# Gated DeltaNet stage: masks ahead of queries on GpSimd, identity and edge masks by bf16 products into PSUM, decay matrix by eight exponentials with a bias

## The reference

```
g = cumsum(log_alpha)
decay = masked_exp(tri_incl, g[:, None] - g[None, :])
L = where(tri_strict, (k * beta) @ k.T * decay, 0)
Tm = inverse of (I + L)
v_new = Tm @ (v * beta) - Tm @ (k * beta * exp(g)) @ S
o = (q * exp(g)) @ S + (q @ k.T * decay) @ v_new
S = S * exp(g_last) + (k * exp(g_last - g)).T @ v_new
```

## Time and profile before

| | before |
|---|---|
| median of 3 runs | 2450.79 us (2449.39 to 2457.24) |
| the profiled execution's own time | 2452.5 us |
| its span, first to last instruction | 2450.7 us |
| PE, PE weight loads, DVE, ACT, POOL busy | 87%, 54%, 60%, 52%, 31% of the span |
| mean granted clock of PE | 0.94 of 2.4 GHz |
| GDN stages | 372.5 to 512.5 us and 1443.5 to 1583.2 us |

### The profile page before, as it was taken

How to read it: one execution, slowest core, us unless ns; L and a number is a source line. 1 busy time by engine, 2 the same in 40 slices (tenths; PEclk the granted TensorE clock), 3 DMA queues, 4 the chain that set the end, 5 groups by cost and what they waited for, 6 DMA issues and landing times.

```text
span 2450.7 us, 54596 instructions
## 1 busy us (share of the span) xinstructions
PE 2143.4 (87%) x23078; PEld 1334.2 (54%) x23078; DVE 1462.0 (60%) x1822; ACT 1284.6 (52%) x1664; POOL 750.9 (31%) x557
## 2 busy tenths in 40 slices
PE   5998987878989999999898878888969999999990
PEld 3765656755565555555765557654644444444440
DVE  2256735559362121215567665386379999999976
ACT  3443753456534242423533654465268877887862
POOL 0422115332314242423232234333122333333321
PEclk8999987998999999999999888898979999999995
DMA  9222990020212222316220000020276677990023
GB/s 276 98 88 73 309 293 11 3 56 4 72 52 86 69 88 66 103 51 176 81 93 24 1 10 3 3 57 22 92 255 212 224 269 277 329 317 35 27 104 137
DMA packets 215385, 278.46 MB, mean 114 GB/s; under 512 B 28177, under 2 KB 188797, under 8 KB 215039
## 3 DMA queue, kind: packets, MB, share of 16 engines
q1 hardware_dynamic: 203776, 243.60, 30.9%
q0 software_dynamic: 8432, 29.89, 3.3%
q10 hardware_dynamic: 2959, 1.83, 0.3%
HBM read 368.35 MB, written 29.11 MB: 162 GB/s over the span
## 4 chain that ended last, share of the span: by engine, by line
PE 52%; issue 16%; DVE 14%; POOL 8%; ACT 7%; DMA 3%; SPq 1%; POOLq 0%; DVEq 0%; ACTq 0%
PE ps L2268 49%; POOL mix L968 5%; DVE arena L1662 2%; DMA wbuf<-in_w_mod 1%; DVE mix L1670 1%; DVE mix L1662 1%; PE ps L2475 1%; ACT arena L1142 1%; DVE mix L1666 1%; DVE const L1662 1%; DVE yg L1662 1%; DVE hT L1662 1%; DVE xT L1662 1%; POOL mix L971 1%; DVE arena L1666 1%
## 5 line engine op out<-in xcount | busy, mean ns | idle before, releaser
L2268 PE MATMUL ps<-hT,mix 128*128 128x512 f16 (+2 forms) x3024 | 380.0, 288 | 25.1 <-DVE hT L1662 15.2
L2268 PE MATMUL ps<-w,xgT 128*128 128x512 f16 x1632 | 365.4, 381 | 7.3 <-DVE w L2163 7.3
L2268 PEld LDWEIGHTS ps<-hT,mix 128*128 128x128 f16 x3024 | 230.0, 99 | 172.8 <-issue 19.5
L2163 DVE SCALAR_TENSOR_TENSOR w<-wst,w 128x2048 f16<-128x2048 f32 x136 | 310.0, 2320 | 22.7 <-ACT w L1523 22.7
L1000 POOL TENSOR_TENSOR a<-aval,a 128x256 f16<-128x256 f32 x68 | 159.0, 2338 | 371.1 <-ACT a L1571 371.1
L2268 PEld LDWEIGHTS ps<-w,xgT 128*128 128x128 f16 x1632 | 157.4, 98 | 186.0 <-issue 10.5
L1523 ACT ACTIVATE w<-wst 128x2048 f16<-128x2048 f32 x136 | 251.5, 1899 | 6.4 <-DMA xs_rows<-htok,slot_i 6.4
L2268 PE MATMUL ps<-mix 128*128 128x512 f16 (+5 forms) x1856 | 203.5, 286 | 14.5 <-POOL mix L971 8.8
L2268 PE MATMUL ps<-hT,arena 128*128 128x128 f16 (+1 forms) x1440 | 201.2, 301 | 1.1 <-DVE const L1662 1.1
L2268 PE MATMUL ps<-w2m,aT 128*128 128x512 f16 x816 | 188.7, 381 | 5.5 <-DVE aT L2201 5.5
L2268 PEld LDWEIGHTS ps<-mix 128*128 128x128 f16 (+3 forms) x1856 | 120.3, 122 | 88.4 <-POOL mix L971 12.4
(11 more groups left out here) (360 smaller groups left out, 3604.5 us busy)
## 6 DMA issues: line engine op xcount, KB each, us to landing
wst<-in_moe_w SPq DMA_DIRECT2D x204, 1024.0 KB
wbuf<-in_w_mod SPq DMA_DIRECT2D x40, 1024.0 KB
wbuf<-in_ffn_w SPq DMA_DIRECT2D x33, 1024.0 KB
wbuf<-in_w_in SPq DMA_DIRECT2D x20, 1024.0 KB
xs_rows<-in_table SPq DMA_DIRECT2D x17, 512.0 KB, 6.3
ys_rows<-yb POOLq DMA_DIRECT2D x17, 512.0 KB, 4.0
wbuf<-in_w_out SPq DMA_DIRECT2D x32, 256.0 KB
xg<-xs_rows POOLq DMA_DIRECT2D x16, 512.0 KB, 5.6
```

What stands on the lines that cost most here:

```text
L2163: v_.scalar_tensor_tensor(out=q[1], in0=staged(s, p), scalar=WS, in1=q[0], op0=ALU.mult, op1=ALU.subtract).then_inc(sg["m_lo13"], 1)
L2268: return mm_(o, w, x, start=first, stop=last, skip_group_check=True)
```

## The change

Four things are changed, all in the GDN stage.

1. GpSimd makes `masked(n)` before `decayed_queries(n)` in every step. `decayed_keys` now waits for grow's slot to be freed.
2. PE adds the edge masks: a job `edge{n}` in grow's slot, after grow has been freed and before G, adds two bf16 products of 128x512 (identity times edge table) to what grow left there. `grow` starts the accumulation only at the first product of each bank. ACT's `rows_of` now frees grow; it no longer waits for DVE.
3. ACT makes the decay matrix by eight exponentials of 128x128 straight from PSUM, each with a column of GC (its sign is now turned) as bias; the last frees `edge{n}`. DVE's `differences` are gone.
4. The identity that the first doubling needs is put into w{n}_1's slot by two bf16 products of 64x512 before the 32 products, which add to it; the first mask table has its sign turned, and ACT copies with the sign +1. The f32 identity product ahead of t{n}_1 is gone.

```diff
-    put("wide", pairs[:, 1:5])
+    put("wide", pairs[:, 1:5] * np.array([-1.0, 1.0, 1.0, 1.0]).reshape(1, 4, 1, 1))
...
-        j += ["3:grow0", "0:G0", "2:KQ0"]
+        j += ["3:grow0", "3:edge0", "0:G0", "2:KQ0"]
...
-                                 (i % 2, "t{}_1", a), (1 - i % 2, "t{}_4", b), (i % 2, "w{}_2", a), (1 - i % 2, "w{}_5", b),
+                                 (i % 2, "t{}_1", a), (1 - i % 2, "t{}_4", b), (2, "edge{}", p), (i % 2, "w{}_2", a), (1 - i % 2, "w{}_5", b),
...
                 def decayed_keys(n):
-                    L.need("eg_ready")
+                    L.done(f"{l}.grow{n}")
...
                     if i < 4:
                         decayed_keys(i + 1)
+                        masked(i + 1)
                         decayed_queries(i + 1)
-                        masked(i + 1)
...
                 def decay(n):
-                    L.need("dm_in")
-                    L.do(a.activation(DM, DM, ACT.Exp), "dm_exp")
+                    j = J(f"edge{n}")
+                    if n:
+                        L.done(J(f"KQ{n - 1}"))
+                    s = L.full(j).rearrange("p (m i) -> p m i", m=8)
+                    for m in range(8):
+                        d, f, r = m // 4, m // 2 % 2, m % 2
+                        c = 4 * chunk(d, n) + 2 * r + f
+                        ins = a.activation(DM[:, m], s[:, m], ACT.Exp, bias=GC[:, d, c:c + 1])
+                        if m < 7:
+                            L.do(ins)
+                    L.free(ins, j)
...
                 def rows_of(n):
-                    L.done(j)
...
-                        L.do(a.activation(EGf.rearrange("p (d r) i -> p d r i", d=2)[h], s[h, f], ACT.Exp),
-                             "eg_ready" if f else None)
+                        ins = a.activation(EGf.rearrange("p (d r) i -> p d r i", d=2)[h], s[h, f], ACT.Exp)
+                        if f == 0:
+                            L.do(ins)
+                    L.free(ins, j)
...
-                        negate(Wc[i % 2], J(f"w{i}_1"), 8)
+                        negate(Wc[i % 2], J(f"w{i}_1"), 8, 1.0)
...
-                        tt(GC, s[:, :, 0], LNB, ALU.subtract)
+                        tt(GC, LNB, s[:, :, 0], ALU.subtract)
...
-                def differences(n):
-
-                    s = wide(f"grow{n}")
-                    for d in range(2):
-                        gg = gate_of(GC, d, chunk(d, n)).unsqueeze(3).broadcast_to([P, 2, 2, P])
-                        tt(per_dir(DM, d), per_dir(s, d), gg, ALU.subtract, job=J(f"grow{n}") if d else None)
-                    for d in range(2):
-                        w = am[:, (1 + 2 * d) * P:(2 + 2 * d) * P].unsqueeze(1).broadcast_to([P, 4, P])
-                        stt(DM[:, 4 * d:4 * d + 4], DM[:, 4 * d:4 * d + 4], 0.0, w, ALU.min, ALU.add, to="dm_in" if d else None)
...
                 def system(n):
-                    L.need("dm_exp")
+                    L.done(J(f"edge{n}"))
...
-                            ins = mm(s[:, at(m)], la2[i][:, d, c:c + 1].broadcast_to([P, P]), inc16[:, d], i == 0, i == 1)
+                            ins = mm(s[:, at(m)], la2[i][:, d, c:c + 1].broadcast_to([P, P]), inc16[:, d], m % 4 + i == 0, i == 1)
...
+                def edge(n):
+                    s = open_(J(f"edge{n}"))
+                    for d in range(2):
+                        ins = mm(s[:, 512 * d:512 * d + 512], identb, edges[:, d].unsqueeze(1).broadcast_to([P, 4, P]),
+                                 False, True)
+                    close(ins, J(f"edge{n}"))
...
                 def gram(n, job):
-                    if job == "G":
-                        L.need("eg_ready")
...
                 def widen(n, v):
+                    if v == 1:
+                        if n >= 2:
+                            pe.wait_ge(sg["t6_act"], 5 * l + n - 1)
+                        s = open_(j)
+                        for b in range(2):
+                            r = slice(64 * b, 64 * b + 64)
+                            mm(s[r, 0:512], identb[r, r], identb[r, r].unsqueeze(1).broadcast_to([64, 8, 64]), True, False)
...
                 def turned(n, v):
-                    if v == 1:
-                        s = open_(J(f"w{n}_{v}"))[:, 512:1024]
-                        mm(s, ident, flat(T64[n % 2]))
...
                     if b_:
                         turned(i - 1, 4)
+                    if p_:
+                        edge(i + 1)
                     if a_:
                         widen(i, 2)
```

More of the change, by code:

```diff
@@ L493, in backbone_kernel @@
             "f_in f_ln lf_ready l2_sq l2_r l2_ready ab_in ab_exp la_ready "
-            "eg_ready dm_in dm_exp kg_ready egl_ready kd_ready qg_ready cs_ready t_ready t_turned lt_ready "
+            "kg_ready egl_ready kd_ready qg_ready cs_ready t_ready t_turned lt_ready "
             "hg_ready lp_hi lp_lo kk_exp kk_ready kw_ready qb_ready qe_ready ke_ready ac_ready ah_ready o_zero o_sq oc_ready oc_sq rs_ready o_ready "
@@ L896, in _ @@
                 pool.wait_ge(sg["g2_out"], 32)
-                decayed_queries(0)
                 pool.wait_ge(sg["near_in"], 48 * (l + 1))
                 masked(0)
+                decayed_queries(0)
                 for i in range(6):
@@ L1239, in diagonal, with negate @@
                         L.do(a.activation(LTc[r], LT[n % 3][r, :, r], ACT.Copy), "ltc_ready" if b else None)
-                def negate(dst, j, m):
+                def negate(dst, j, m, sign=-1.0):
                     s = L.full(j)[:, 0:m * dst.shape[2]].rearrange("p (m i) -> p m i", m=m)
-                    L.free(a.activation(dst, s, ACT.Copy, scale=-1.0), j)
+                    L.free(a.activation(dst, s, ACT.Copy, scale=sign), j)
                 def inverse(n, v):
@@ L2016, in weigh @@
                     tt(KE[u % 2], E_, KTt[n % 2][:, x].unsqueeze(1).broadcast_to([P, 7, P]), ALU.mult, to="ke_ready")
-                differences(0)
                 system(0)
@@ L2026, in _ @@
                         remainder(i - 2)
-                    if p_:
-                        differences(i + 1)
                     if a_:
@@ L2528, in tiles @@
                             r = slice(64 * b, 64 * b + 64)
-                            ins = mm(s[r, 64 * m:64 * m + 64], lhs[r, m], rhs[r, m], first)
+                            ins = mm(s[r, 64 * m:64 * m + 64], lhs[r, m], rhs[r, m], first and m == 0)
                     return ins
@@ L2539, in widen @@
                         L.done(J(f"t{n}_{v - 1}"))
-                    if v == 1 and n >= 2:
-                        pe.wait_ge(sg["t6_act"], 5 * l + n - 1)
-                    close(tiles(open_(j), masked_tiles(n, v), T64[n % 2]), j)
+                    close(tiles(open_(j), masked_tiles(n, v), T64[n % 2], v > 1), j)
                 def turned(n, v):
                     j = J(f"t{n}_{v}")
-                    if v == 1:
-                        s = open_(J(f"w{n}_{v}"))[:, 512:1024]
-                        mm(s, ident, flat(T64[n % 2]))
                     L.done(J(f"w{n}_{v}"))
@@ L2552, in turned @@
                         pe.wait_ge(sg["t_turned"], 3 * (5 * l + n) + v - 1)
-                    close(tiles(open_(j)[:, 512:1024], Tt64[n % 2], Wc[n % 2], False), j)
+                    close(tiles(open_(j)[:, 512:1024], Tt64[n % 2], Wc[n % 2], v == 1), j)
                 def pair_down(n):
@@ L2688, in _ @@
                 grow(0)
+                edge(0)
                 gram(0, "G")
```

## The result

| | before | after |
|---|---|---|
| median of 4 runs | 2450.97 us (2449.39 to 2457.24) | 2485.03 us (2472.73 to 2492.13) |
| ratio | | 1.0113, 95% interval 1.0087 to 1.0139 |
| the profiled execution | 2452.5 us, span 2450.7 | 2488.65 us, span 2486.9 |
| mean granted clock | 0.940 | 0.929 |

The change makes the kernel slower, which is the forecast side, but by more than the forecast 16 us: the two medians differ by 34 us, and the recorded ratio of 1.0113 would be 28 us. The median lies 5 us above the range's upper end of 2480; by the ratio the time lies just inside it (2450.97 x 1.0113 = 2478.7).

A forecast was written before the change was run, and what follows sets the result against it. The GDN stage was taken as bound by engines waiting for one another, none full. Terms summed to +7.9 us per layer, +15.8 for both: 2452.5 + 15.8 - 1.7 = 2467 us, range 2456 to 2480.

The forecast's parts named there:

- edge wait: PE's edge products wait for ACT's rows_of and delay w{i}_2 and its negation: +1.65 us per step, bounds 1.4 and 2.2.
- exponentials: On ACT's stretch of the chain, eight small exponentials take 3.15 us instead of 1.07: +2.1 us in steps 0 to 3.
- steps 0 to 3: GDN stage parts, each from w{i}_1's start on PE, also preparing a following chunk; forecast together 5 to 10 us longer.
- both losing parts: Edge wait, 1.65 us, and exponentials, 2.1 us, together 3.75 us in a step.
- Identity: f32 product before t{i}_1 goes: 1.1 to 1.5 us less in steps 0 to 4; bf16 pair costs 0.3 on three.
- The rival on the clock: New PE gaps before edge and G lower the granted clock: +4 us per layer, 2475 us; chance 0.15.
- Masks first: GpSimd's masks no longer wait behind queries: at most 2.2 us back, net -1.2 us in steps 2 and 3 each.
- the port: DVE instructions with SBUF operands slow down beside GpSimd's masks: 1.0 us lost in steps 2 and 3, bounds 0 and 2.2.
- rival B: GpSimd and DVE port conflict eats the masks' gain, 2.2 us lost per step: +2.4 per layer, 2472 us; chance 0.13.
- The stages' sum: All terms of the GDN stage together: +7.9 us per layer, +15.8 us for both layers.
- Nothing afterwards absorbs a shift: After the GDN stage the fetch of w_out waits for its last product, so the +15.8 us reaches the total.

The follow-up runs named there:

- e3: The kernel before with only the edge products on PE and the eight exponentials in place of DVE's differences; 2485.21 us, ratio 1.0140.
- f0: The changed kernel run and profiled once more, unaltered; 2481.71 us, ratio to before 1.0121.
- e2: The kernel before with only the identity changed, to two bf16 products ahead of w_1; 2451.77 us, ratio 0.9981.
- e1: The kernel before with only GpSimd's masks put ahead of its queries; 2448.94 us, ratio 0.9977.
- g2: e4 with DVE's turn of the third inverse and 64-block copies moved ahead of the state's update; 2434.11 us, ratio to before 0.9915.
- e4: The kernel before with both masks first and the bf16 identity, without edge products and eight exponentials; 2443.43 us, ratio 0.9961.
- g1: The changed kernel with six unused bf16 products added on PE in the wait before the edge products; 2471.09 us, ratio to before 1.0071.

## Why the prediction was right or wrong

**The side: right, by its own steps.** The edge wait and the exponentials cost more than identity and masks gain. The signs named for it are there: PE idle 2.00 us by ACT, 80 activations at 0.367, eight in 3.17 us (3.15 in the working), no f32 identity, w3_1 and w4_1 released by DVE, the subtraction at 1.64, step 4 shorter. One was missed: steps 0 to 3 together are 13.5 and 12.4 us longer, not 5 to 10. e3 alone measures 15.0 of 15.6 us per layer; as its two layers are 5 us apart, an agreement to 0.6 is partly luck.

**Edge wait: the sum right, the split off.** Taking it away brings 11.1 and 7.6 us in the stages, the term was 1.65 x 4 = 6.6. The 1.65 holds the wait with products at the high clock, and there it is nearly right. This is the negation of w0_2 in e3, then in f0:

```profile
394.99 0.60 ACT L1254 ACTIVATE const<-ps 128x512 f32<-128x512 f32 x1 [1.85 <-PE ps L2265]
403.04 0.60 ACT L1254 ACTIVATE const<-ps 128x512 f32<-128x512 f32 x1 [2.11 <-PE ps L2265]
```

ACT pauses 1.85 us with both products at the high clock (the working had 1.7), 2.11 in f0, where w0_2 ran in part at the low one, and 3.10 in after, with both at the low one, above the bound of 2.2. The wait of PE before them is the same in all three, 2.00 or 2.01 us. The steps differ: for both losing parts e3 pays 4.4, 4.8, 3.7 and 2.3 us in steps 0 to 3 of layer 1 (22.2, 26.1, 29.5 and 29.9 long) where 3.75 stood for each, 15.2 where 15.0 stood, and layer 2's four give 13.8.

**Identity: the term that failed most.** Forecast was -6.2 + 0.9 = -5.3 per layer; e2 measured -0.2 and -0.9. The chain was read rightly: w4_1 started 1.12 us earlier, and the steps with before's clock are shorter by 0.7 to 1.2 us. The new pair of bf16 products took 0.40 us at the high clock, where 0.3 stood. What was left out is the clock at which the rest then runs: over the stage it was 0.82 and 0.83, and the products behind the waits took 3.68 us instead of 3.05. The rival on the clock looked at gaps that the change adds and not at work that it takes out between existing ones; e3, which has the gaps and keeps the work, lost no clock.

**Masks first: over-sized.** Net -1.2 was forecast in steps 2 and 3, out of 2.2 less 1.0 for the port. The port took 1.6, which is rival B between its value and the forecast's. 0.57 us were left in step 2 and 0.55 in step 3, and e1's stages are 0.7 and 0 shorter; its median, 0.2% below before's, can't tell this from the forecast's 4.8 us. What was late next was named rightly (blocks64), but the prediction stopped at it: g2 shows that the real gain of masks first lies behind it.

**The stages' sum** was +7.9 per layer and is +11.2 in the mean of after's two: 22.4 us against 15.8. e3 and e4 say why: costs 0.6 below the forecast, gains 4.1 below.

**Outside the stages** the prediction had nothing, and the profiled execution has 13.8 us (f0 12.6). "Nothing afterwards absorbs a shift" held; that nothing is added there did not. The first stage starts at 378.5 and 379.5 us in after and f0, at 378.6 and 378.4 in g1 and g2, and between 370.7 and 374.4 in before and all the others. The clock up to there is 0.91 or 0.92 in the late ones and 0.94 or 0.95 in all others, with nothing edited there. The time at the low level is 65 us there in after and 47 in before, and 73 against 57 between the stages, so the lost time goes with the clock. Why the clock is lower is open. It isn't the losing parts, since e3 starts at 372.0 and g2, which has none of them, at 378.4. Of the stretch between the stages part may be chance: over the fourteen profiles it is 933.1 to 943.1 us.

## What to carry to other kernels

When two engines end almost together, look at what the second one waits for before you price the first: masks first alone brought 0.2%, DVE's order alone cost 0.9%, both together gained 0.85%, with the bf16 identity in the kernel too, which no run separates from them. Before you write into a PSUM slot in the middle of a chain, ask who frees it: one job moved behind the work it had blocked was worth more than half of the loss here. And work removed from an engine that waits was worth its length here only where the products around it kept their clock; look at the granted clock of the stretch, not of the whole span.

## What the hardware showed that was not expected

- Eight independent 128x128 activations take 3.17 us if each waits for the one before and 2.17 without: from one start to the next (3.17 - 0.37) / 7 = 0.40 us against (2.17 - 0.38) / 7 = 0.26.
- With six added bf16 products in a wait the granted clock of a stage was 0.88 and 0.87 instead of 0.80 to 0.85 (after and f0), and the stages were 2.3 us shorter with more work. Without the f32 product it was 0.82 and 0.83 instead of 0.86 and 0.87, and the stages gained 0.2 and 0.9 us of 5.3.
- Beside GpSimd's masks the DVE instructions with two operands in SBUF grow (0.69 to 1.64, 0.42 to 1.07), but not the one that began 0.04 us before the first mask (0.69), nor those that read PSUM or one buffer; DVE is busy 69.1 us in before's first stage and 72.6 in e1's.
- A program can begin a stage 6 us later, in stretches where its instructions are those of another program, and do so again in a second profile of it (378.5 and 379.5).
